# Projecting tokens 256 to 768 before their root is known, in a one-core hybrid encoder layer

## The chip, the cores and the metric

The kernel runs as one program on one core of a Trainium2 chip. The metric is the device time of one execution in microseconds (us); lower is better. The engines are named as in the profile: PE (TensorE, matrix products; PEld is its loading of weights), DVE (VectorE), ACT (ScalarE), POOL (GpSimd) and SP (SyncE, which here issues DMAs).

## What is computed

The reference is one encoder layer over two sequences with the same weights: 256 tokens of a prompt and 1024 tokens of a sample, 1280 in all, 1024 features each. The part around the change is the first step of the layer, the normalisation and the first projection:

```python
def rmsnorm(x, w):
    xf = x.astype(F32)
    y = xf * lax.rsqrt(jnp.mean(xf * xf, axis=-1, keepdims=True) + EPS)
    return (y * w.astype(F32)).astype(x.dtype)

h = rmsnorm(x, pre_mix_norm)
z = h @ w_in + b_in
aq, ak, av, mq, mk, mv, mo, mi, mf, gates = jnp.split(z, SPLIT_POINTS, axis=-1)
ya = windowed_gqa_attention(aq, ak, av, attn_sink)
ym = bidirectional_mlstm(mq, mk, mv, mo, mi, mf, mlstm_norm)
```

Behind it follow a gated merge of both branches, an output projection with a second norm, and a gated feed-forward network with a short convolution. Since the root of a token is one factor for all its features, `rmsnorm(x) @ w` is the same as `(x * w_norm) @ w` times the root of that token; the bias comes after.

## The kernel before

Tokens lie on the free axis and features on the partitions. The 1024 features are `KT = 8` tiles of 128. Every matrix product is made in two-part numbers: an operand is split into a high part (`unit_h`, `ht_h`) and what is left of it (`unit_l`, `ht_l`), and a product of one tile is three matmuls: high by high, low by high, high by low. Weights come in units of 128 output columns (512 KB, tile `unit_raw`), five slots of them, in which unit n lies in slot n mod 5. ACT makes a unit's high part (`unit_hi`, line 2030, semaphore `s_wh`) and POOL its low part (`take_low`, line 1396, semaphore `s_split`).

The program of every engine is an order written out by hand; engines meet only at semaphores. The tokens are worked in three chunks, `CHUNKS`: 0 is tokens 0 to 256, 1 is 256 to 768, 2 is 768 to 1280. The list `START` gives the order of the first groups on PE. For each chunk these are the gate columns of the mLSTM ("if", unit 0, 16 columns that count) and then the groups of units 1 to 4, which are the queries and keys of the first mLSTM head. A group's number is 3u + c for unit u + 1 and chunk c. In `if_group` the first of these groups (two in chunk 1) runs beside the gate columns, tile by tile, as the tiles of `ht` become ready. After `START` come the ten blocks of values and output gates (`vo_group`), 128 tokens each, whose moving operand is units 5 to 8 at once (slots 0 to 3), and which therefore need all four.

A chunk is prepared as follows. SP loads `xs`. ACT squares the eight tiles (`square_x`, line 2013), DVE adds the squares (lines 2422, 2429, 2432), PE sums them over the partitions with a matrix of ones (`sum_squares`, lines 3310 and 3314), ACT makes the root (`rstd_x`, lines 2018 and 2020). Then, tile by tile, DVE multiplies x by the norm's weight and the root (line 2477), ACT makes the high part `ht_h` (`x_hi`, line 2026), and DVE subtracts it to give `ht_l` (line 2482). `s_htd` counts the finished tiles.

After the third chunk DVE clears row tiles for the gate arithmetic (lines 2486 to 2492; these tiles share their memory with `xs`), adds up the gate rows of chunk 2 (`if_sum(2)`, line 2445), and goes on with the gates' scans. On SP the loads of units 5 and 6 wait only for a free slot, but those of units 7 and 8 stand behind the copies of the gate rows:

```python
m_first[4]()
m_first[5]()
sp.wait_ge(ev_dve, GROUPS[("if", 0, 2)][3])
sp.wait_ge(p_row, 1)
for d in range(2):
    sp.dma_start(r_li[32 * d:32 * d + 4, :], r_if[4 * d:4 * d + 4, :]).then_inc(p_in, 16)
    sp.dma_start(r_f[32 * d:32 * d + 4, :], r_if[8 + 4 * d:12 + 4 * d, :]).then_inc(p_in, 16)
for k in range(6, M_UNITS):
    m_first[k]()
```

(`m_first[k]` loads unit k + 1. `ev_dve` at that count is `if_sum(2)`, and `p_row` 1 is the last of the clears.) On ACT the high part of unit 8 stands behind that of unit 7, behind two activations of the gate rows (lines 2103 and 2105, which wait for DVE's line 2500), and behind one eviction. The first block of values waits with `pe.wait_ge(s_wh, M_UNITS)` for the high parts of all eight units.

Of the kernel before, what the change touches and what calls it, by code (L numbers as in the profile page):

```python
# [24 lines left out]
P = 128  # L25
# [140 lines left out]
HI_HEADS = M_UNITS + 4  # L166
# [40 lines left out]
START = [("if", 0, 0)] + [("M", 0, 3 * u) for u in range(4)]  # L207
START += [("if", 0, 1)] + [("M", 0, 3 * u + 1) for u in range(4)]
START += [("if", 0, 2)] + [("M", 0, 3 * u + 2) for u in range(4)]
START_BANKS = [0, 1, 5, 6, 7]  # L210

SUM_BEFORE = [9, 10]

BESIDE_IF = [[0], [1, 4], [2]]
# [209 lines left out]
def group_tables():  # L424

    order = list(START)
    out = {}
    for h in range(HEADS):
        order += [("M", h, g) for g in range(0 if h else 12, 22)]
        order += [("A", h, g) for g in (range(21) if h < HEADS - 1 else [*range(15), *LATE])]  # L430
    count = {"act": 0, "dve": 0}
    last = {}
    for i, key in enumerate(order):
        bank = START_BANKS[i % 5] if i < len(START) else i % 2
        eng = "dve" if key[0] == "if" or key[0] == "M" and key[2] >= 12 else "act"
# [23 lines left out]
def build(nc, w, wdn, xt, cols, bvo, sink, outs):  # L459
# [22 lines left out]
    unit_raw = at("unit_raw", 20480, [P, SLOTS, KT, P])  # L482

# [58 lines left out]
    sq_x = at("sq_x", 81920, [P, KT, T])  # L542
    ones0 = at("ones0", 196288, [P, P])
# [85 lines left out]
    s_xl = [sem(f"x_landed{c}") for c in range(3)]  # L629
    s_cols = sem("cols_landed")  # L630
    s_cst = sem("consts_dve")
# [10 lines left out]
    s_wh1 = sem("first_unit_hi")  # L642
# [259 lines left out]
    with ctx_block as block:  # L902
# [3 lines left out]
        def _(sp):  # L906
# [447 lines left out]
        def _(pool):  # L1354
            nc.gpsimd.memset(ident[:], 0.0)
# [26 lines left out]
            def take_rest(n, done, half):  # L1382
                slot = n % SLOTS
                pool.wait_ge(s_wh, M_UNITS + done)
# [6 lines left out]
            def take_low(n):  # L1391

                pool.wait_ge(*((s_wh1, 1) if n == 1 else (s_wh, n)))
                step = 2 if n < SLOTS else KT
                for k in range(0, KT, step):
# [5 lines left out]
            low = slice(HD, P)  # L1401
            nc.gpsimd.tensor_tensor(unit_h[:, 0, :, low], unit_raw[:, 0, :, low], unit_h[:, 0, :, low].bitcast(F32),
                                    ALU.subtract).then_inc(s_split, 1)
            for n in range(1, 1 + M_UNITS):
                take_low(n)
# [595 lines left out]
        def _(act):  # L2001
            nc.scalar.preload_act_table_set("natural_log_exp_and_others")

            act.dma_start(colt[:, 0:NCOL], cols[:]).then_inc(s_cols, 16)
            act.dma_start(sinks[:], sink[0:1, :].to_broadcast([P, 16])).then_inc(s_cols, 16)

            def square_x(c, k):
                a, b = CHUNKS[c]
                act.wait_ge(s_xl[c], 16)
                if c:  # L2010
                    act.wait_ge(s_sqm, c)
# [3 lines left out]
            def rstd_x(c):  # L2015
                stat = ps[:, 2 + c, 0:CHUNKS[c][1] - CHUNKS[c][0]]
                act.wait_ge(s_sqm, c + 1)
                nc.scalar.activation(stat, stat, ACT.Ln, bias=eps_col, scale=1.0 / D)
                act.drain()
                nc.scalar.activation(stat, stat, ACT.Exp, scale=-0.5).then_inc(s_rs, 1)  # L2020

            def x_hi(c, tiles=range(KT)):
                a, b = CHUNKS[c]
                for k in tiles:
                    act.wait_ge(s_xn, c * KT + k + 1)
# [21 lines left out]
            def evac_m(g, h, shift=0):  # L2047
# [17 lines left out]
            act.wait_ge(s_unit[2], 16)
            for k in range(4):
                x_hi(0, [k])
                last = nc.scalar.activation(unit_h[:, 2, 2 * k:2 * k + 2], unit_raw[:, 2, 2 * k:2 * k + 2], ACT.Identity)
            last.then_inc(s_wh, 1)
            x_hi(0, range(4, 7))  # L2070
            square_x(1, 0)
            x_hi(0, [7])
            square_x(1, 1)
            square_x(1, 2)
            unit_hi(3)
            for k in range(3, KT):
                square_x(1, k)
            unit_hi(4)
            act.wait_ge(s_cols, 32)
# [3 lines left out]
            rstd_x(1)  # L2083
            x_hi(1)
            evac_m(6, 0)
            evac_m(9, 0)
            for k in range(KT):
                square_x(2, k)
            evac_if(1)
            evac_m(1, 0)  # L2090
            evac_m(4, 0)
            rstd_x(2)
            evac_m(7, 0)
            x_hi(2)
            evac_m(10, 0)
# [23 lines left out]
            act.wait_ge(p_80, 32)  # L2119
# [291 lines left out]
        def _(dve):  # L2411
            V = nc.vector
            V.memset(ones0[:], 1.0)
            V.memset(eps_col, EPS).then_inc(s_cst, 1)
            for r in range(16):
                V.memset(slope8[:, r:r + 1], -(2.0 ** (-8.0 * (r + 1) / 16)) * HD ** 0.5)
            def add_squares_x(c):

                t = slice(CHUNKS[2][0], CHUNKS[2][0] + CHUNKS[c][1] - CHUNKS[c][0])
                for k in range(1, KT):  # L2420
                    dve.wait_ge(s_sq, c * KT + k + 1)
                    V.tensor_tensor(sq_x[:, 0, t], sq_x[:, 0, t], sq_x[:, k, t], ALU.add)
                    dve.drain()
                dve.sem_inc(s_sqa, 1)

            for k in range(0, KT, 2):
                dve.wait_ge(s_sq, k + 2)
                t = slice(CHUNKS[2][0], CHUNKS[2][0] + SEQ_A)
                V.tensor_tensor(sq_x[:, k, t], sq_x[:, k, t], sq_x[:, k + 1, t], ALU.add)
                if k % 4 == 2:  # L2430
                    dve.drain()
                    V.tensor_tensor(sq_x[:, k - 2, t], sq_x[:, k - 2, t], sq_x[:, k, t], ALU.add).then_inc(s_sqa, 1)
            dve.wait_ge(s_cols, 32)
# [7 lines left out]
            def if_sum(c):  # L2441
                a, b = CHUNKS[c]
                rows = slice(0, 4 * HEADS)
                dve.wait_ge(s_ifl, c + 1)
# [17 lines left out]
            for c, (a, b) in enumerate(CHUNKS):  # L2462
                if c:
                    add_squares_x(c)
                    if_sum(c - 1)
                if c == 1:
                    dve.wait_ge(s_cstp, 1)

                    V.scalar_tensor_tensor(absrel[:], absrel[:], -1.0, absrel[:], ALU.mult, ALU.max)
                    dve.drain()  # L2470
                    V.tensor_scalar(y_st.rearrange("p a b t -> p (a b t)")[:, 0:3 * P], absrel[:], float(P), BIG, ALU.is_gt, ALU.mult)
                    dve.drain()
                    V.tensor_tensor(absrel[:], absrel[:], y_st.rearrange("p a b t -> p (a b t)")[:, 0:3 * P], ALU.max)
                dve.wait_ge(s_rs, c + 1)
                for k in range(KT + 1):
                    if k < KT:
                        V.scalar_tensor_tensor(xs[:, k, a:b], xs[:, k, a:b], colt[:, C_PRE + k:C_PRE + k + 1],
                                               ps[:, 2 + c, 0:b - a], ALU.mult, ALU.mult).then_inc(s_xn, 1)
                    if k:

                        dve.wait_ge(s_xh, c * KT + k)
                        V.tensor_tensor(ht_l[:, k - 1, a:b], xs[:, k - 1, a:b], ht_h[:, k - 1, a:b].bitcast(F32),
                                        ALU.subtract).then_inc(s_htd, 1)

# [115 lines left out]
            def gated(i, h):  # L2600
# [11 lines left out]
                last.then_inc(m_ss, 1)  # L2612

# [657 lines left out]
        def _(pe):  # L3271
# [31 lines left out]
            pe.wait_ge(s_cst, 1)  # L3303
            def sum_squares(c):
                a, b = CHUNKS[c]
                first = CHUNKS[2][0]
                if c == 0:
                    for p in range(2):
                        pe.wait_ge(s_sqa, p + 1)
# [3 lines left out]
                pe.wait_ge(s_sqa, 2 + c)  # L3313
# [769 lines left out]
```

## Time and profile before

| | before |
|---|---|
| median of 3 runs | 2379.15 us (2378.35 to 2379.68) |
| span of the profiled execution, first to last instruction | 2375.6 us |
| PE busy | 2342.6 us, 99% of the span |
| DVE, POOL, ACT busy | 65%, 54%, 38% of the span |
| PE's longest idle stretches | 8.83 us at the start, 2.73 us before the first projection |

The page gives the profiled execution's time as its span alone; the median of the runs lies 3.55 us above it. The chain of work that ended last is PE for 88% of the span. All that the change touches lies in the first 145 us.

### The profile page before, as it was taken

To read this page: it belongs to the slowest core of one execution; us is meant where nothing else is said; L and a number is where in the kernel's file an instruction comes from. 1 tells how busy PE (TensorE), PEld (TensorE's weight loads), DVE (VectorE), ACT (ScalarE), POOL (GpSimd) and SP (SyncE) were. 2 spreads that over 40 slices of the span, in tenths; PEclk is the share of its full clock that TensorE was granted. 3 is DMA by queue.
4 is the path that set the end of the run, shared out by engine and by line. 5 is a ranking of instruction groups with operands and counts; after the bars stand their busy time and mean duration, and the time that the engine had idled before them with its cause. 6 is when DMAs were issued, how large, how long until landed. Compare 5 with 4: busy or idle time off the path is not lost.

```text
span 2375.6 us, 37136 instructions
## 1 busy us (share of the span) xinstructions
PE 2342.6 (99%) x13734; PEld 2120.7 (89%) x13734; DVE 1546.4 (65%) x2699; ACT 909.6 (38%) x1862; POOL 1279.8 (54%) x1556
## 2 busy tenths in 40 slices
PE   7999999999999999999999999999999999999998
PEld 6888888888888888888888899999999999989887
DVE  6734467554674547755786642999778777965447
ACT  5212443224442244324644112554333434552443
POOL 3365522555225641346452548797455555986576
PEclk9999999999999999999999999999999999999999
DMA  3133211321113311223454443332443434488873
GB/s 139 52 104 94 69 38 27 109 92 54 36 40 99 102 52 32 70 79 123 128 169 158 138 155 117 122 122 89 153 147 131 165 130 138 144 279 271 282 238 120
DMA packets 186956, 285.66 MB, mean 120 GB/s; under 512 B 14344, under 2 KB 126824, under 8 KB 186776
## 3 DMA queue, kind: packets, MB, share of 16 engines
q1 hardware_dynamic: 139320, 241.99, 30.7%
q10 hardware_dynamic: 47456, 41.31, 5.9%
q8 instruction: 109, 1.79, 0.3%
q14 instruction: 71, 0.58, 0.1%
HBM read 203.48 MB, written 79.68 MB: 119 GB/s over the span
## 4 chain that ended last, share of the span: by engine, by line
PE 88%; DVE 5%; DVEq 2%; POOL 2%; ACT 1%; DMA 1%; issue 1%; ACTq 0%; POOLq 0%
PE ps L3285 15%; PE ps L3287 15%; PE ps L3286 15%; PE ps L3840 4%; PE ps L3842 4%; PE ps L3841 4%; PE ps L3352 3%; PE ps L3350 3%; PE ps L3351 3%; PE ps L3300 3%; PE ps L3296 3%; PE ps L3297 3%; PE ps L3549 2%; PE ps L3457 2%; PE ps L3569 2%; PE ps L3583 1%
## 5 line engine op out<-in xcount | busy, mean ns | idle before, releaser
L3285 PE MATMUL ps<-ht_h,unit_h 128*128 128x512 f32 (+1 forms) x1408 | 503.7, 358 | 0.8 <-POOL unit_l L1396 0.6
L3287 PE MATMUL ps<-ht_h,unit_l 128*128 128x512 f32 (+1 forms) x1408 | 498.4, 354 | 0.0
L3286 PE MATMUL ps<-ht_l,unit_h 128*128 128x512 f32 (+1 forms) x1408 | 498.1, 354 | 0.0
L1374 POOL TENSOR_TENSOR unit_h<-unit_raw,colt 128x256 fp32r<-128x256 f32 x320 | 208.5, 683 | 275.1 <-DMA unit_raw<-w 274.8
L3285 PEld LDWEIGHTS ps<-ht_h,unit_h 128*128 128x128 f32 x1408 | 266.2, 189 | 37.2 <-POOL unit_l L1396 1.6
L3287 PEld LDWEIGHTS ps<-ht_h,unit_l 128*128 128x128 f32 x1408 | 265.9, 189 | 37.4
L3286 PEld LDWEIGHTS ps<-ht_l,unit_h 128*128 128x128 f32 x1408 | 266.2, 189 | 35.1 <-issue 0.2
L1378 POOL TENSOR_TENSOR unit_l<-unit_raw,unit_h 128x256 fp32r<-128x256 f32 x320 | 246.8, 803 | 11.7 <-issue 0.4
L1546 POOL TENSOR_TENSOR unit_l<-unit_raw,unit_h 128x256 fp32r<-128x256 f32 x164 | 157.8, 987 | 91.9 <-DVE unit_raw L2944 91.9
L1546 POOL TENSOR_TENSOR sum_l<-sum_raw,sum_h 128x256 fp32r<-128x256 f32 x132 | 138.9, 1073 | 91.9 <-DVE sum_raw L2951 78.6
L1467 POOL TENSOR_TENSOR v_high<-v_raw,colt 128x256 fp32r<-128x256 f32 x40 | 27.1, 677 | 231.3 <-DVE o_st L2459 231.3
L2273 ACT ACTIVATE prob<-prob,small 128x384 f32<-128x384 f32 (+1 forms) x160 | 89.8, 563 | 113.0 <-DVE small L2661 112.9
L1586 POOL TENSOR_TENSOR block_l<-block_raw,block_h 128x256 fp32r<-128x256 f32 x120 | 107.2, 933 | 45.5 <-ACT block_h L1899 45.5
L3296 PE MATMUL ps<-operands,unit_h 128*128 128x320 f32 (+1 forms) x420 | 125.5, 311 | 1.0 <-ACT kept_products L1819 1.0
L3297 PE MATMUL ps<-operands,unit_h 128*128 128x320 f32 (+1 forms) x420 | 124.9, 309 | 0.0
L2648 DVE SCALAR_TENSOR_TENSOR prob<-absrel,slope,ps 128x384 f32<-128x384 f32 (+1 forms) x160 | 79.0, 556 | 68.1 <-PE ps L3569 39.0
L3350 PE MATMUL ps<-unit_h,ht_h 128*128 128x512 f32 x312 | 123.2, 395 | 0.0
L3352 PE MATMUL ps<-unit_h,ht_l 128*128 128x512 f32 x312 | 121.6, 390 | 0.0
L3351 PE MATMUL ps<-unit_l,ht_h 128*128 128x512 f32 x312 | 121.5, 389 | 0.0
L1577 POOL TENSOR_TENSOR down_l<-down_raw,down_h 128x256 fp32r<-128x256 f32 x88 | 82.0, 967 | 33.3 <-DVE s_stage L3082 26.7
L3285 PE MATMUL ps<-operands,unit_h 128*128 128x322 f32 (+1 forms) x320 | 99.7, 311 | 0.3
L3287 PE MATMUL ps<-operands,unit_l 128*128 128x322 f32 (+1 forms) x320 | 99.5, 311 | 0.0
(417 smaller groups left out, 6463.7 us busy)
## 6 DMA issues: line engine op xcount, KB each, us to landing
unit_raw<-w SPq DMA_DIRECT2D x149, 512.0 KB, 4.0
bw<-exponent_rows_scratch ACTq DMA_DIRECT2D x40, 256.0 KB, 3.7
down_raw<-wdn SPq DMA_DIRECT2D x24, 384.0 KB, 4.1
side_raw<-side_sum_scratch SPq DMA_DIRECT2D x24, 384.0 KB, 5.9
block_raw<-weight_sum_scratch SPq DMA_DIRECT2D x16, 576.0 KB, 4.3
gate_scratch<-g_st SPq DMA_DIRECT2D x28, 256.0 KB, 3.6
stage<-f_scratch SPq DMA_DIRECT2D x28, 256.0 KB, 3.0
side_sum_scratch<-stage SPq DMA_DIRECT2D x14, 512.0 KB, 2.9
```

The lines of the kernel that those rows point to most:

```text
L1374: nc.gpsimd.tensor_tensor(unit_h[:, slot, k:k + 2], unit_raw[:, slot, k:k + 2], one_col.unsqueeze(2).to_broadcast([P, 2, P]), ALU.mult)
L1378: last = nc.gpsimd.tensor_tensor(unit_l[:, slot, k:k + 2], unit_raw[:, slot, k:k + 2], unit_h[:, slot, k:k + 2].bitcast(F32), ALU.subtract)
L1546: last = nc.gpsimd.tensor_tensor(lo[:, k:k + 2], raw[:, k:k + 2], hi[:, k:k + 2].bitcast(F32), ALU.subtract)
L1586: last = nc.gpsimd.tensor_tensor(blk_l[n][:, a:b], blk_raw[n][:, a:b], blk_h[n][:, a:b].bitcast(F32), ALU.subtract)
L3285: mm(out_ap, wh, hi(k + k_first), start=first and k == 0, stop=False, skip_group_check=skip)
L3286: mm(out_ap, wh, lo(k + k_first), start=False, stop=False, skip_group_check=skip)
L3287: ins = mm(out_ap, wl, hi(k + k_first), start=False, stop=last and k == kts - 1, skip_group_check=skip)
L3296: mm(out_ap, unit[0](k), hi(k), start=first and k == 0, stop=False, skip_group_check=skip)
L3297: mm(out_ap, unit[0](k), lo(k), start=False, stop=False, skip_group_check=skip)
L3350: mm(ps[:, bank, :], ht_h[:, k, t], unit_h[:, 0:4, k], start=k == 0, stop=False)
L3351: mm(ps[:, bank, :], ht_h[:, k, t], unit_l[:, 0:4, k], start=False, stop=False)
L3352: ins = mm(ps[:, bank, :], ht_l[:, k, t], unit_h[:, 0:4, k], start=False, stop=k == KT - 1)
```

## The change

Chunk 1 is now the first to be projected, then chunk 0, then chunk 2 (`RAW_FIRST`). Its tiles are loaded in four pairs, ahead of everything but the gate weights, and are split into high and low part without the root: x times the norm's weight only. The gate columns and groups 1, 4, 7 and 10 (`RAW_M`) are made from these raw tiles; DVE multiplies the root into them as it evicts them (`raw_m`, `raw_if`) and ACT adds the bias afterwards (`raw_bias`). The squares of chunk 1 and 0 are added by DVE as before, in tiles of their own for chunk 1; those of chunk 2 are added by POOL. The normalised split of chunk 1, which the blocks of values and everything later read, is made after that of chunk 2 (`normed(1)` behind `normed(2)`). The gate weights are loaded as 16 columns per tile instead of 128. The core of the diff:

```diff
+HI_START = M_UNITS + 1
+RAW_FIRST = [1, 0, 2]
+NORMED = {0: 1, 2: 2, 1: 3}
+START = []
+for _c in RAW_FIRST:
+    START += [("if", 0, _c)] + [("M", 0, 3 * u + _c) for u in range(4)]
+RAW_M = [1, 4, 7, 10]
+SUM_BEFORE = {7: 1, 10: 0, 6: 2}
+BESIDE_IF = [[0], [1], [2]]
...
+            def load_first(n):
+                a, b = CHUNKS[1]
+                sp.dma_start(xs[:, 2 * n:2 * n + 2, a:b], xt[2 * n:2 * n + 2, :, a:b].rearrange("k p t -> p k t")
+                             ).then_inc(s_xf[n], 16)
+            sp.dma_start(if_raw[:], w[0, :, 0:KT * 4 * HEADS].rearrange("p (k c) -> p k c", k=KT)
+                         ).then_inc(s_unit[0], 16)
+            load_first(0)
+            m_first[0]()
+            for n in range(1, 4):
+                load_first(n)
+            m_first[1]()
             load_x(0)
-            load(lambda hh: 0, 0)
-            m_first[0]()
-            m_first[1]()
-            load_x(1)
             m_first[2]()
             m_first[3]()
             load_x(2)
...
+            third = slice(CHUNKS[2][0], T)
+            for k in range(1, KT):
+                pool.wait_ge(s_sq, 2 * KT + k + 1)
+                nc.gpsimd.tensor_tensor(sq_x[:, 0, third], sq_x[:, 0, third], sq_x[:, k, third], ALU.add)
+                pool.drain()
+            pool.sem_inc(s_sqa, 1)
...
+            def raw_hi(k):
+                a, b = CHUNKS[1]
+                act.wait_ge(s_xf[k // 2], 16 if k > 1 else 32)
+                nc.scalar.activation(ht_h[:, k, a:b], xs[:, k, a:b], ACT.Identity, scale=colt[:, C_PRE + k:C_PRE + k + 1]
+                                     ).then_inc(s_xh, 1)
...
+            rstd_x(1)
+            unit_hi(4)
             rstd_x(0)
+            for k in range(KT):
                 x_hi(0, [k])
+                square_x(2, k)
+            act.wait_ge(a_sel, 1)
+            for g in RAW_M:
+                raw_bias(g)
             evac_if(0)
             evac_m(0, 0)
             evac_m(3, 0)
+            rstd_x(2)
+            x_hi(2)
             evac_m(6, 0)
             evac_m(9, 0)
+            x_hi(1)
             evac_if(2)
             evac_m(2, 0)
             unit_hi(5)
...
+            for k in range(KT):
+                dve.wait_ge(s_xh, k + 1)
+                V.scalar_tensor_tensor(ht_l[:, k, first], xs[:, k, first], colt[:, C_PRE + k:C_PRE + k + 1],
+                                       ht_h[:, k, first].bitcast(F32), ALU.mult, ALU.subtract).then_inc(s_htd, 1)
...
+            def raw_m(g):
+                u = g // 3
+                dve.wait_ge(d_done, GROUPS[("M", 0, g)][0] + 1)
+                V.scalar_tensor_tensor((mq_t if u < 2 else mk_t)[:, u % 2, first], ps[:, GROUPS[("M", 0, g)][1], :],
+                                       1.0 if u < 2 else DH ** -0.5, r_raw[:], ALU.mult, ALU.mult).then_inc(ev_dve, 1)
...
+            raw_if()
+            for g in RAW_M[:2]:
+                raw_m(g)
+            normed(0)
+            for g in RAW_M[2:]:
+                raw_m(g)
+            if_sum(0)
+            normed(2)
+            normed(1)
+            dve.wait_ge(s_cstp, 2)
...
-                    pe.wait_ge(s_wh, M_UNITS)
+                    pe.wait_ge(s_wh, HI_START)
...
+                if blk == 2 and h + shift == 0:
+                    pe.wait_ge(s_htd, 4 * KT)
```

Three places of the orders are shown. The first is DVE's program at the end of the preparation. In the kernel before, the last low part of chunk 2 is followed at once by the clears and by `if_sum(2)` (the `r_if` row; the row behind it waits for the copies of the gate rows):

```order
L2482 TENSOR_TENSOR ht_l<-xs,ht_h 128x512 x2
L2486 MEMSET v_high 128x10x2
L2487 MEMSET r_li 36x1280
L2488 MEMSET r_f 36x1280
L2489 MEMSET r_m 36x1280
L2490 MEMSET r_mp 36x10
L2492 MEMSET r_rst 36x1280
L2445 SCALAR_TENSOR_TENSOR r_if<-ps,colt,r_if 16x512
```

In the changed kernel the same clears and the same `if_sum(2)` on DVE stand behind the whole of `normed(1)`, of which the last two rows are shown (`r_raw` is the root of chunk 1), and behind the three operations on `absrel`:

```order
L2494 SCALAR_TENSOR_TENSOR xs<-xs,colt,r_raw 128x512
L2499 TENSOR_TENSOR ht_l<-xs,ht_h 128x512 x2
L2544 SCALAR_TENSOR_TENSOR absrel<-absrel 128x384
L2546 TENSOR_SCALAR y_st<-absrel 128x384
L2548 TENSOR_TENSOR absrel<-absrel,y_st 128x384
L2551 MEMSET v_high 128x10x2
L2552 MEMSET r_li 36x1280
L2553 MEMSET r_f 36x1280
L2554 MEMSET r_m 36x1280
L2555 MEMSET r_mp 36x10
L2557 MEMSET r_rst 36x1280
L2470 SCALAR_TENSOR_TENSOR r_if<-ps,colt,r_if 16x512
```

So 16 operations of 128x512 and the three on `absrel` now lie between the end of chunk 2's split and the gate rows; in the kernel before they were done ahead of chunk 2. The second place is SP's queue from its start, in the kernel before:

```order
L909 DMA xs<-xt 128x8x256
L917 DMA unit_raw<-w 128x1024 x3
L909 DMA xs<-xt 128x8x512
L917 DMA unit_raw<-w 128x1024 x2
L909 DMA xs<-xt 128x8x512
L967 DMA bias_vo<-bvo 128x512
L917 DMA unit_raw<-w 128x1024 x2
L973 DMA r_li<-r_if 4x1280
L974 DMA r_f<-r_if 4x1280
L973 DMA r_li<-r_if 4x1280
L974 DMA r_f<-r_if 4x1280
L917 DMA unit_raw<-w 128x1024 x2
```

In the changed kernel the head of SP's queue is another, up to the load of chunk 2; from `bias_vo` on the rows follow one another as before, units 7 and 8 again behind the four copies of the gate rows:

```order
L970 DMA if_raw<-w 128x128
L967 DMA xs<-xt 128x2x512
L923 DMA unit_raw<-w 128x1024
L967 DMA xs<-xt 128x2x512 x3
L923 DMA unit_raw<-w 128x1024
L915 DMA xs<-xt 128x8x256
L923 DMA unit_raw<-w 128x1024 x2
L915 DMA xs<-xt 128x8x512
```

Two tiles of chunk 1 now come second in the queue, and chunk 0 sixth. The third place is POOL's program after its constants, in the kernel before: the low part of the gate weights, of units 1 to 4 and of units 5 to 8, and then its work on the first values:

```order
L1402 TENSOR_TENSOR unit_h<-unit_raw,unit_h 128x8x64
L1396 TENSOR_TENSOR unit_l<-unit_raw,unit_h 128x256 x16
L1396 TENSOR_TENSOR unit_l<-unit_raw,unit_h 128x1024 x4
L1467 TENSOR_TENSOR v_high<-v_raw,colt 128x256
L1469 TENSOR_TENSOR v_low<-v_raw,v_high 128x256
```

In the changed kernel seven additions of squares stand between units 4 and 5 on POOL:

```order
L1416 TENSOR_TENSOR unit_h<-if_raw,unit_h 128x8x16
L1411 TENSOR_TENSOR unit_l<-unit_raw,unit_h 128x256 x16
L1423 TENSOR_TENSOR sq_x<-sq_x 128x512 x7
L1411 TENSOR_TENSOR unit_l<-unit_raw,unit_h 128x1024 x4
L1489 TENSOR_TENSOR v_high<-v_raw,colt 128x256
```

The seven additions of 128x512 are new to POOL; on DVE, which made them before, they are gone.

## Rows read from the trace of the kernel before

**Rows 1.** The page's first line.
```profile
span 2375.6 us, 37136 instructions
```

**Rows 2.** Timeline of PE: start, us, engine, line, operation, count, idle before and its releaser.
```profile
8.83 2.35 PE L3310 MATMUL ps<-sq_x,ones 128*128 128x256 f32 x4 [8.83 <-DVE sq_x L2432]
13.91 0.55 PE L3381 MATMUL ps<-ht_h,unit_h 128*128 128x256 f32 x1 [2.73 <-DVE ht_l L2482]
...
20.02 0.31 PE L3381 MATMUL ps<-ht_h,unit_h 128*128 128x256 f32 x1
...
20.52 1.12 PE L3398 MATMUL ps<-ht_h,unit_l 128*128 128x256 f32 x8
21.48 0.28 PE L3285 MATMUL ps<-ht_h,unit_h 128*128 128x256 f32 x1
...
52.80 1.02 PE L3314 MATMUL ps<-sq_x,ones 128*128 128x512 f32 x2
...
59.14 0.39 PE L3381 MATMUL ps<-ht_h,unit_h 128*128 128x512 f32 x1
...
84.53 0.39 PE L3340 MATMUL ps<-unit_h,ht_h 128*128 128x512 f32 x1
...
88.68 0.50 PE L3344 MATMUL ps<-unit_l,ht_h 128*128 128x512 f32 x1 [0.37 <-POOL unit_l L1396]
```

**Rows 3.** SP's queue: start, us of issue, line, DMA; units 7 and 8 last.
```profile
0.74 0.44 SPq L909 DMA_DIRECT2D xs<-xt  x1
...
71.99 0.74 SPq L973 DMA_DIRECT2D r_li<-r_if  x1
...
74.65 4.96 SPq L917 DMA_DIRECT2D unit_raw<-w  x2
```

**Rows 4.** Timeline of ACT: the high part of unit 8.
```profile
82.72 1.06 ACT L2030 ACTIVATE unit_h<-unit_raw 128x1024 fp32r<-128x1024 f32 x1
```

**Rows 5.** Timeline of DVE: `absrel`, chunk 2's split from first to last, `if_sum(2)`.
```profile
27.63 0.79 DVE L2469 SCALAR_TENSOR_TENSOR absrel<-absrel 128x384 f32<-128x384 f32 x1
...
29.29 0.56 DVE L2473 TENSOR_TENSOR absrel<-absrel,y_st 128x384 f32<-128x384 f32 x1
...
55.20 1.41 DVE L2477 SCALAR_TENSOR_TENSOR xs<-xs,colt,ps 128x512 f32<-128x512 f32 x2 [7.04 <-ACT ps L2020]
...
64.22 1.47 DVE L2482 TENSOR_TENSOR ht_l<-xs,ht_h 128x512 fp32r<-128x512 f32 x2
...
71.35 0.62 DVE L2445 SCALAR_TENSOR_TENSOR r_if<-ps,colt,r_if 16x512 f32<-16x512 f32 x1
```

**Rows 6.** DMA issues of the page (KB each, us to landing), then of the first 90 us.
```profile
unit_raw<-w SPq DMA_DIRECT2D x149, 512.0 KB, 4.0
...
xs<-xt SPq DMA_DIRECT2D x1, 1024.0 KB, 5.6
```

**Rows 7.** Groups by shape, ACT's high part of a 512-wide tile: busy, mean ns.
```profile
L2026 ACT ACTIVATE ht_h<-xs 128x512 fp32r<-128x512 f32 x16 | 10.1, 632 | 8.9 <-DVE xs L2477 8.8
```

**Rows 8.** Timeline of DVE: chunk 0's split, additions of squares beside POOL and alone.
```profile
12.21 0.87 DVE L2477 SCALAR_TENSOR_TENSOR xs<-xs,colt,ps 128x256 f32<-128x256 f32 x2 [0.74 <-ACT ps L2020]
...
18.16 1.43 DVE L2482 TENSOR_TENSOR ht_l<-xs,ht_h 128x256 fp32r<-128x256 f32 x2
...
21.23 5.47 DVE L2422 TENSOR_TENSOR sq_x<-sq_x 128x512 f32<-128x512 f32 x5 [0.27 <-ACT sq_x L2013]
...
42.01 5.30 DVE L2422 TENSOR_TENSOR sq_x<-sq_x 128x512 f32<-128x512 f32 x7 [1.08 <-ACT sq_x L2013]
```

**Rows 9.** Timeline of POOL from 10 to 29 us.
```profile
10.15 1.29 POOL L1402 TENSOR_TENSOR unit_h<-unit_raw,unit_h 128x512 fp32r<-128x512 f32 x1 [7.43 <-ACT unit_h L2030]
11.40 2.96 POOL L1396 TENSOR_TENSOR unit_l<-unit_raw,unit_h 128x256 fp32r<-128x256 f32 x4
15.86 3.45 POOL L1396 TENSOR_TENSOR unit_l<-unit_raw,unit_h 128x256 fp32r<-128x256 f32 x4 [1.50 <-ACT unit_h L2068]
20.76 8.24 POOL L1396 TENSOR_TENSOR unit_l<-unit_raw,unit_h 128x256 fp32r<-128x256 f32 x8 [1.44 <-ACT unit_h L2030]
```

More of the change, by code:

```diff
@@ L434, in group_tables @@
         bank = START_BANKS[i % 5] if i < len(START) else i % 2
-        eng = "dve" if key[0] == "if" or key[0] == "M" and key[2] >= 12 else "act"
+        raw = key[1] == 0 and key[2] in RAW_M
+        eng = "dve" if key[0] == "if" or key[0] == "M" and (key[2] >= 12 or raw) else "act"
         count[eng] += 1
@@ L2460, in evac_vo, with normed @@
                                 ALU.add).then_inc(ev_dve, 1)
[L2462 to L2474, printed above, removed]
+            def normed(c, between=None):
+                a, b = CHUNKS[c]
+                root = r_raw[:] if c == 1 else ps[:, 2 + c, 0:b - a]
+                dve.wait_ge(s_rs, RAW_FIRST.index(c) + 1)
                 for k in range(KT + 1):
@@ L2483, in _, with raw_if @@
                                         ALU.subtract).then_inc(s_htd, 1)
+            def raw_if():
+                rows = slice(0, 4 * HEADS)
+                dve.wait_ge(s_ifl, 1)
+                V.tensor_tensor(r_if[rows, first], ps[rows, GROUPS[("if", 0, 1)][1], :], r_if[rows, first], ALU.add)
+                dve.wait_ge(s_rs, 1)
+                dve.drain()
+                V.tensor_tensor(r_if[rows, first], r_if[rows, first], r_raw[rows], ALU.mult)
+                dve.drain()
+                V.tensor_scalar(r_if[rows, first], r_if[rows, first], colt[rows, C_IF:C_IF + 1], None, ALU.add
+                                ).then_inc(ev_dve, 1)
@@ new lines, in _ @@
+            dve.sem_inc(s_sqa, 1)
+            for k in range(0, KT, 2):
+                dve.wait_ge(s_sq, KT + k + 2)
+                t = slice(CHUNKS[2][0], CHUNKS[2][0] + SEQ_A)
+                V.tensor_tensor(sq_x[:, k, t], sq_x[:, k, t], sq_x[:, k + 1, t], ALU.add)
+                if k % 4 == 2:
+                    dve.drain()
+                    V.tensor_tensor(sq_x[:, k - 2, t], sq_x[:, k - 2, t], sq_x[:, k, t], ALU.add).then_inc(s_sqa, 1)
+            raw_if()
+            for g in RAW_M[:2]:
+                raw_m(g)
@@ L2612, in gated @@
                 last.then_inc(m_ss, 1)
+            dve.wait_ge(p_80, 48)
             def mlstm(h, dense):
@@ L3399, in if_group @@
                     ins.then_inc(d_done, 1)
-            sum_squares(0)
+                    return
+                for k in range(KT):
+                    pe.wait_ge(s_htd, KT * NORMED[c] + k + 1)
+                    gates(k)
+                    beside_hi(k)
+                    ins = mm(beside, wl(k), ht_h[:, k, a:b], start=False, stop=k == KT - 1)
+                ins.then_inc(d_done, 1)
             for kind, _, g in START:
@@ L3996, in sl @@
         return slice(a, a + P)
-    gates = np.zeros((D, P), w_in.dtype)
-    for first in (0, HD):
-        gates[:, first:first + 4 * HEADS] = w_in[:, off_if:off_if + 4 * HEADS]
-    units = [unit(gates, slice(0, P))]
+    gates = np.zeros((P, KT * P), w_in.dtype)
+    gates[:, 0:KT * 4 * HEADS] = (w_in[:, off_if:off_if + 4 * HEADS].reshape(KT, P, 4 * HEADS).transpose(1, 0, 2)
+                                  .reshape(P, KT * 4 * HEADS))
+    units = [gates]
     for h in range(HEADS):
```

202 lines of the change are left out of this document (98 added, 104 removed).

## The prediction

> **What bounds the kernel now.** I read the page first: PE is busy nearly throughout a span of 2375.6 us [rows 1], so only two things can move the time here: work taken off PE, of which the change takes none (112 projection matmuls per chunk before and after), and time in which PE waits or runs slowly. Next I read PE's own timeline of the first 90 us. It waits 8.83 us for the squares of chunk 0 and 2.73 us more for the first split tile. The first projection starts at 13.91 us, and the next 28 matmuls of 256 columns take 0.218 us each, up to 20.02 us; from there eight take 0.96 us, 0.12 each [rows 2]. 256 columns in 0.21 us is the lower of TensorE's two clock levels, 1.2 GHz, in 0.11 the upper, 2.4 GHz. So the start costs 13.9 us of idleness, and a slow stretch of 6.1 us, half of which (3.05 us) is lost. After that PE is nearly always fed: chunk 2 runs its 112 matmuls from 59.14 to 84.53 us, 0.2267 each, and the first block of values follows at once, with one wait of 0.37 us [rows 2].
>
> Then I looked at what has to be there at 84.53. The first block needs the high part of units 5 to 8; that of unit 8 is ready at 82.72 + 1.06 = 83.78 [rows 4], only 0.75 us early. It is last on ACT behind the gate rows, and its load is last on SP behind their copies, which start at 71.99 [rows 3], as `if_sum(2)` ends on DVE (71.35 + 0.62 = 71.97) [rows 5]. So there is a chain of 83.78 - 71.97 = 11.81 us from `if_sum(2)` to the first block, and in the kernel before it was nearly the bound. This is the place that decides.
>
> **The change, part by part.** *The start.* The first pair of raw tiles is 512 KB. A lone load of that size lands after 4.0 us and one of 1 MB after 5.6 [rows 6], 1.6 us per further 512 KB. It is second in the queue, after the first issue at 0.74 of 0.44 us [rows 3], with 64 KB of gate weights and the column constants beside it, for which I add 0.5: it lands at about 5.7. ACT's high part takes 0.63 [rows 7], DVE's low part 0.7 (half of 1.41 for two of that shape) [rows 5]. PE starts at about 7.1 instead of 13.91. The other tiles come in faster (two per 1.6 us) than a cold PE uses them (four matmuls of 0.43 each), so they don't hold it.
>
> *Chunk 1.* Up to the sum for chunk 0 stand 88 matmuls (19.95 us), the sum for chunk 1 (0.9, from a row of 1.02 whose end overlaps), that for chunk 0 (about 1.0: a row of 2.35 in the slow stretch, halved and cut in the same way), and the slow start, which I take as long as in the row, 3.05 lost: 7.1 + 19.95 + 0.9 + 1.0 + 3.05 = 32.0. Group 10 ends 24 matmuls later, at 37.4.
>
> *Chunk 0.* DVE starts its split 1.03 us after the sum (8.83 + 2.35 to 12.21) [rows 2, 8], at 33.0. In the row its eight tiles end after 7.38 us (18.16 + 1.43) [rows 8], which would be ahead of PE. But POOL now adds the squares of chunk 2 meanwhile: seven additions of 128x512, 1.29 us each by the nearest row alone [rows 9]. What DVE and POOL do to each other can be read: POOL's 128x256 pieces take 0.74 us beside an idle DVE, 0.86 beside DVE's split, 1.03 beside DVE's additions, and DVE's additions of 128x512 take 0.76 (5.30 for 7) with POOL idle and 1.09 (5.47 for 5) with POOL at work [rows 8, 9]. POOL's two sizes give 0.55 us of transfer per 256 elements and 0.19 around it; 0.55 + 0.53 for DVE's 512 elements is the 1.09 of the row: they take turns. So one low part (about 0.35) waits for one addition (1.10): with a little between, 1.5 us a tile. The additions can start when two squares are there (two times 0.9 after a first 0.5), at 35.3; tile 2 is ready at 36.9, tile 7 at 44.4. PE, free at 37.4, finishes tile 7 at 45.0, group 3 (24 x 0.12) at 47.9 and the sum for chunk 2 at **E = 48.8**. If they did not take turns, PE would come through at 45.1 and E would be 46.0; I take the first, since both rows fit it, and keep the other as the lower end.
>
> The Trainium skill, "SBUF — State Buffer", section "Who interferes with whom", says that a VectorE instruction with two inputs in SBUF and a GpSimd instruction that reads SBUF exclude one another for a whole instruction. The 1.09 us agrees. By that rule E is 48.8, without it 46.0: it speaks against moving these additions to POOL.
>
> *From E on.* PE still has groups 6 and 9 (48 x 0.12) and the 112 matmuls of chunk 2 (25.4): 31.15 us, so it is through at 80.0, 4.5 us earlier than 84.53. DVE starts the split of chunk 2 1.38 us after the sum (52.80 + 1.02 to 55.20) and needs 10.49 us for it (to 64.22 + 1.47 = 65.69) [rows 2, 5]. Then it now makes the split of chunk 1, the same 16 operations, another 10.49 (its root comes from SBUF, not PSUM; no row shows that form in this width, and I take the same). Then `absrel`, 2.22 (27.63 to 29.29 + 0.56). Then the clears and `if_sum(2)`, 6.28 (65.69 to 71.97) [rows 5]. They cannot go ahead of it, since the cleared rows lie in the memory of `xs`. So `if_sum(2)` ends at 48.8 + 1.38 + 20.98 + 2.22 + 6.28 = **79.7**, 7.7 us later than before. Behind it wait on SP the four copies and the loads of units 7 and 8 (whose slots are free long before), on ACT the gate rows and the high part of unit 8, and on PE the first block. With the same 11.81 us that block starts at **91.5**, not 84.53: 6.95 us late. PE is idle for 11.5 us before it.
>
> *The clock.* The only such idleness in the trace is that of the start, and PE came out of it at the lower level. I take the same 6.1 us again, 3.05 lost. If the clock held, the block's 16 high-part matmuls would take 3.6 us, while unit 8's low part is ready 88.68 - 83.78 = 4.9 us after its high part [rows 2, 4]: a wait of 1.2 us. So this term is 3.05 or 1.2, and the old wait of 0.37 is gone in either case. The Trainium skill, "TensorE: Matmul & The Clock Gate", section on the HAM clock gate, says that the slow level is the default and activity releases it; no row here shows it for an idle stretch in mid-kernel.
>
> *Hidden at no cost.* Four evictions with the root on DVE (0.7 each), two of them between the splits of chunk 0 and 2, are over by 46 while DVE waits until 50; without that cover 1.4 us. Four bias activations and the gate rows' extra operations lie beside PE's work likewise. The second split is over at 71, far ahead of the third block of values that waits for it. Later consumers of the gate rows are delayed less (7.7) than PE, so they keep their distance.
>
> **Sum.** 6.95 + 3.05 - 0.37 = 9.6 us, nothing behind it gives it back as PE is the chain. Span 2385.2; the runs' median lies 3.55 above the span, so **2388.8 us**, 0.4% slower.
>
> **Rivals.** *The start's gain is kept.* If units 7 and 8 came in time, PE would enter the first block at 80.0: 4.5 us faster, 2374.6, or with E = 46.0 7.3 us, 2371.8. For it speaks that units 5 and 6 and all slots are indeed early; it decides once `if_sum(2)` ends by 80.0 - 11.8 = 68.2, which is 11.5 us earlier than worked out, more than the whole second split (10.5). Chance 0.05. *Neither contention nor a slow second start.* E = 46.0 gives the first block at 88.7, 4.15 late, and 1.2 - 0.37 for the low part: 5.0 us, 2384.1. If the first slow stretch is also half as long, 1.5 less: 2382.6, inside 0.2%. Chance 0.20, of which 0.15 falls inside. *POOL is slower still.* At 2.06 us per addition (twice 1.03 [rows 9]) the sum for chunk 2 waits until 49.7, E is 50.6, and the time 2390.6. Chance 0.14. *The raw tiles come late.* If the pair lands only with two further loads (3.2 us), everything shifts by that: 2392.0. Chance 0.06. My forecast has the remaining 0.55.
>
> **The numbers.** I call 0.2% (4.8 us) what this kernel's runs can tell from no change; they spread by 1.3 us. Slower by more: 0.55 + 0.05 + 0.14 + 0.06 = 0.80. Within: 0.15. Faster: 0.05. The range reaches from the low case inside 0.2% (2382.6) to the late tiles: 2382.5 to 2392.
>
> **What would show it.** In the changed kernel's timeline: PE's first projection near 7 us, without one of the two waits of before; the seven additions on POOL at 1.4 to 1.6 us each, with DVE's low parts of chunk 0 between them; PE through with chunk 2 near 80; `if_sum(2)` ending near 79.7, SP's copies right behind it, and one wait of PE of about 11 us, released by ACT's high part of unit 8, and slow matmuls behind it. I am wrong if that wait is short: if `if_sum(2)` ends before 70, or if the first block does not stand behind unit 8. A first projection later than 9 us would break the first step, and a sum for chunk 2 done by 46 that of POOL and DVE taking turns.

## The result and the profile after

The changed kernel takes 2387.62 us (median of 4 runs, 2386.28 to 2390.09), the kernel before, measured beside it, 2379.41 (2378.35 to 2379.98): 1.0038 times as long, 95% interval 1.0026 to 1.0049. It is 8.2 us slower; 2388.8 was predicted.

The page's first line, beside [rows 1], and the waits of PE in the first 100 us (releaser, us in total, times, longest):

```profile
span 2384.5 us, 37150 instructions
...
PE ps L3417 <- ACT unit_h L2055: 10.5, 1, 10.5
PE ps L3453 <- DVE ht_l L2457: 9.2, 1, 9.2
PE ps L3453 <- DVE ht_l L2499: 1.7, 3, 0.6
```

In the first block of values, where the kernel before waited 0.37 us, stands a wait of 10.5. PE's timeline, which answers to [rows 2]:

```profile
9.20 0.77 PE L3453 MATMUL ps<-ht_h,unit_h 128*128 128x512 f32 x1 [9.20 <-DVE ht_l L2457]
...
12.64 0.40 PE L3453 MATMUL ps<-ht_h,unit_h 128*128 128x512 f32 x1
...
44.82 0.39 PE L3453 MATMUL ps<-ht_h,unit_h 128*128 128x256 f32 x1 [0.56 <-DVE ht_l L2499]
...
48.39 1.02 PE L3385 MATMUL ps<-sq_x,ones 128*128 128x512 f32 x2
...
80.19 0.39 PE L3354 MATMUL ps<-ht_h,unit_l 128*128 128x512 f32 x1
91.08 0.77 PE L3417 MATMUL ps<-unit_h,ht_h 128*128 128x512 f32 x1 [10.50 <-ACT unit_h L2055]
...
94.54 0.39 PE L3417 MATMUL ps<-unit_h,ht_h 128*128 128x512 f32 x1
...
96.38 1.98 PE L3421 MATMUL ps<-unit_l,ht_h 128*128 128x512 f32 x8
```

The first projection starts 4.7 us earlier than before (9.20 for 13.91), the sum for chunk 2 comes 4.4 us earlier (48.39 for 52.80), and the last matmul of chunk 2 starts at 80.19, 4.1 us earlier (84.30 before). Then PE stands still, and the first block of values begins 6.55 us later than before (91.08 for 84.53). The rest of the chain tells why; this is the chain of work that ended last, cut to 70 to 100 us (start, us, what):

```profile
71.08 0.69 DVE ht_l L2499
...
76.40 1.12 DVE r_m L2554
...
79.03 0.55 DVE r_if L2470
79.60 0.74 SPq L987
...
82.26 3.56 DMA unit_raw<-w
85.84 1.06 ACT unit_h L2055
86.90 1.18 ACT r_b L2139
88.15 1.27 ACT r_b L2141
89.42 0.57 ACT mk_t L2062
89.99 0.95 ACT unit_h L2055
91.08 0.77 PE ps L3417
```

Read upwards: the block waits for the high part of unit 8 (89.99). That stands on ACT behind two activations of the gate rows and an eviction, those behind the high part of unit 7 (85.84); the loads of units 7 and 8 were issued on SP only behind the four copies of the gate rows; the copies waited for `if_sum(2)` (79.03); and `if_sum(2)` stands on DVE behind the clears and the end of the second split (71.08 + 0.69). From the end of `if_sum(2)` (79.57) to the end of that high part it is 89.89 + 1.04 - 79.57 = 11.4 us by ACT's timeline, nearly as long as before (11.81 by [rows 4, 5]).

### The profile page after: what moved, and what is told of

Its sections match the earlier page's. It is cut to its first block, busy times and chain, and to the rows that moved or that the text cites. A ratio compares the mean times of both kernels' runs of the same rounds, so it can differ in the third digit from the quotient of the medians.

```text
span 2384.5 us, 37150 instructions
## 1 busy us (share of the span) xinstructions
PE 2343.5 (98%) x13734; PEld 2121.5 (89%) x13734; DVE 1554.7 (65%) x2706; ACT 913.1 (38%) x1867; POOL 1289.1 (54%) x1564
## 4 chain that ended last, share of the span: by engine, by line
PE 89%; DVE 6%; DVEq 2%; POOL 1%; ACT 1%; DMA 1%; issue 0%; SPq 0%; ACTq 0%
PE ps L3352 15%; PE ps L3354 15%; PE ps L3353 15%; PE ps L3923 4%; PE ps L3924 4%; PE ps L3925 4%; PE ps L3367 3%; PE ps L3363 3%; PE ps L3364 3%; PE ps L3429 3%; PE ps L3431 3%; PE ps L3430 3%; PE ps L3632 2%; PE ps L3540 2%; PE ps L3652 2%; PE ps L3666 1%
## 5 line engine op out<-in xcount | busy, mean ns | idle before, releaser
L3352 PE MATMUL ps<-ht_h,unit_h 128*128 128x512 f32 (+1 forms) x1392 | 497.3, 357 | 0.3 <-issue 0.3
L3354 PE MATMUL ps<-ht_h,unit_l 128*128 128x512 f32 (+1 forms) x1392 | 492.2, 354 | 0.0
L3353 PE MATMUL ps<-ht_l,unit_h 128*128 128x512 f32 (+1 forms) x1392 | 491.9, 353 | 0.0
L1393 POOL TENSOR_TENSOR unit_l<-unit_raw,unit_h 128x256 fp32r<-128x256 f32 x320 | 246.1, 799 | 11.4
L3110 DVE TENSOR_TENSOR side<-side_raw,side 128x1536 fp32r<-128x1536 f32 (+2 forms) x40 | 65.2, 1662 | 53.0 <-ACT side L1833 52.9
```

The lines of the kernel that those rows point to most:

```text
L1393: last = nc.gpsimd.tensor_tensor(unit_l[:, slot, k:k + 2], unit_raw[:, slot, k:k + 2], unit_h[:, slot, k:k + 2].bitcast(F32), ALU.subtract)
L3352: mm(out_ap, wh, hi(k + k_first), start=first and k == 0, stop=False, skip_group_check=skip)
L3353: mm(out_ap, wh, lo(k + k_first), start=False, stop=False, skip_group_check=skip)
L3354: ins = mm(out_ap, wl, hi(k + k_first), start=False, stop=last and k == kts - 1, skip_group_check=skip)
```

## The experiments

Three theories went into the first four runs. **A**, that of the prediction: the second split makes the gate rows late, and they hold up unit 8 in two queues, SP's (its load) and ACT's (its high part). **B**: SP's queue alone does it. **C**: the loss lies in the start, in DVE and POOL holding each other up, or in the clock. The kernel before was measured again beside the first four runs (26 executions) and beside the last four (28); its median is 2378.93 us both times. Each experiment starts from the changed kernel.

**Loads first.** Units 7 and 8 are loaded ahead of the copies.

```diff
+            for k in range(6, M_UNITS):
+                m_first[k]()
             sp.wait_ge(ev_dve, GROUPS[("if", 0, 2)][3])
...
-            for k in range(6, M_UNITS):
-                m_first[k]()
```

> The loads of units 7 and 8 are issued on SP ahead of the wait for the gate rows; nothing else is changed. Theory A (the late gate rows hold unit 8's high part on ACT as well, behind the two activations of the gate rows): the loads land near 75 and 79 us, but the first block of values still starts near 91 and the time stays within 1 us of the changed kernel's 2387.6. Rival B (the queue of loads on SP is what holds the block): the wait of 10.5 us shrinks to a few us and the time falls by 8 to 12 us, to about 2377. Rival C (the loss lies in the start, the contention or the clock): no change, and the wait stays as long.

Measured: 2387.17 us, 1.0036 times before (1.0023 to 1.0049), no gain. ACT's timeline of this run:

```profile
77.47 1.06 ACT L2055 ACTIVATE unit_h<-unit_raw 128x1024 fp32r<-128x1024 f32 x1
89.54 1.27 ACT L2139 ACTIVATE r_b<-r_b 36x1280 f32<-36x1280 f32 x1 [11.01 <-DVE r_b L2565]
90.88 1.27 ACT L2141 ACTIVATE r_b<-r_b 36x1280 f32<-36x1280 f32 x1
92.05 0.67 ACT L2062 ACTIVATE mk_t<-ps,hc 128x512 f32<-128x512 f32 x1
92.62 1.04 ACT L2055 ACTIVATE unit_h<-unit_raw 128x1024 fp32r<-128x1024 f32 x1
```

Unit 7 is through at 78.5. Then ACT is idle for 11.01 us, waiting for the gate rows, and unit 8 is behind them. PE's wait is 10.51 us. B falls: once the load is early, the second queue holds it as long. That SP's queue would hold the block by itself too is read from the chain above, not tried.

**Loads and unit 8.** Also on ACT, unit 8 goes ahead of the gate rows.

```diff
+            evac_m(8, 0)
+            unit_hi(8)
             act.wait_ge(p_row, 2)
             nc.scalar.activation(r_b[0:36], r_b[0:36], ACT.Exp, scale=-1.0)
...
-            evac_m(8, 0)
-            unit_hi(8)
             evac_m(11, 0)
```

> As e1, and on ACT the high part of unit 8 and one eviction are put ahead of the two activations of the gate rows. Theory A: the first block starts at about 80.4, as PE is through with chunk 2, without a slow stretch. But DVE evicts the first block only behind the gates' scans, at about 99 to 100, as in the changed kernel, so PE waits some 8 us before the third block, which needs that bank; net gain only 3 to 4 us, time about 2384. Rival B or C: if the gates' chain holds nothing else, the whole wait and the slow restart are saved, 12 us, time about 2375.5.

Measured: 2382.89 us, 1.0016 (1.0007 to 1.0026). The 10.5 us are gone: chunk 2 runs into the first block at 81.17 without a wait. Another wait has come, PE's waits from 78 us on in this run:

```profile
PE ps L3429 <- DVE o_st L2484: 6.6, 1, 6.6
```

The third block (98.80) needs a bank that DVE evicts only after the gate rows' scans, so the late rows hold PE in a third queue. Gained against the changed kernel: 4.7 us; the trace accounts for 10.5 - 6.6 = 3.9, since behind either wait eight or nine matmuls run at 0.43 us.

**Early evictions.** In addition, DVE evicts the first blocks between the steps of the gate rows.

```diff
+            evac_vo(0, 0)
             dve.wait_ge(p_act, 1)
...
             V.tensor_tensor_scan(r_b[0:4], r_rst[0:4], r_f[0:4], 0.0, ALU.mult, ALU.add)
+            evac_vo(1, 0)
...
-                evac_vo(n, 0)
+                evac_vo(n + 2, 0)
...
-            evac_vo(2, 0)
+            evac_vo(4, 0)
```

> As e2, and on DVE the evictions of the first five blocks of values are moved ahead between the gates' steps (the first one behind the step before the softplus, the second behind the first scan, and so on). Theory A: no wait at the first or third block; PE runs 10.7 us ahead of the changed kernel and saves the slow restart of 1.7, until the transposes in the last block, which need the gates' rows at about 133 while PE is there at about 129: a wait of 3 to 4 us. Net gain 8 to 9 us, time about 2379, equal to the kernel before. If the gates' chain were not the cause: no gain over e2.

Measured: 2376.37 us, 0.9987 (0.9977 to 0.9996). All waits of PE from 78 to 180 us in this run:

```profile
PE ps L3501 <- ACT decay L2157: 1.0, 1, 1.0
```

11.25 us less than the changed kernel; the trace accounts for 10.5 (wait) + 1.6 (slow matmuls behind it) - 1.0 = 11.1. The spans of the two profiled executions differ by less, 9.6 us, since the clock cost them different amounts elsewhere (the sum and the last section). With these three moves the change, second split and all, is 2.6 us faster than the kernel before. The moves were not tried on the kernel before, but there PE has only one wait of 0.4 us between 78 and 180 us for them to save.

**No second split.** The second split is left out, and the blocks of chunk 1 read raw tiles, without the root (`normed(1)`, its high parts and the wait for them are missing).

```diff
             normed(2)
-            normed(1)
```

> The changed kernel without the second, normalised split of tokens 256 to 768: DVE's 16 operations and ACT's 8 are left out, so all that follows reads the raw tiles of these tokens. Theory A: the gate rows of chunk 2 end 10.5 us earlier, near 69, the first block starts near 80.9 (69.1 + 11.8), PE waits under 1 us there, and the time falls by 11 to 12 us to about 2376, faster than the kernel before by the gain at the start. Rival C: the second split is hidden behind PE's work; leaving it out changes less than 2 us.

Measured: 2377.22 us, 0.9993 (0.9983 to 1.0002), 10.4 us less than the changed kernel. PE's waits from 78 us on:

```profile
PE ps L3418 <- POOL unit_l L1411: 1.1, 1, 1.1
PE ps L3414 <- ACT unit_h L2055: 0.2, 1, 0.2
```

`if_sum(2)` ends at 69.53 in this run, and the block follows chunk 2 with 0.23 us between. So the second split is the cause; the queues of the first three runs are how it reaches PE. C falls as the main cause, since neither the third nor the fourth run touched the start.

**One addition.** POOL makes only the last of the seven additions of squares (six squares are left out of the root of chunk 2).

```diff
-            for k in range(1, KT):
+            for k in range(KT - 1, KT):
```

> The changed kernel with only the last of POOL's seven square additions (six squares are left out of the root of chunk 2). Theory A says DVE's low parts of chunk 0 wait a whole POOL addition each: without six of them the tiles follow one another at about 0.85 us instead of 1.44, the last tile of chunk 0 is ready near 41.4 instead of 44.8, PE does not wait for it (it is through with the tiles at 42.8 instead of 45.4), and everything behind, the wait of 10.5 us for unit 8 included, comes 2.6 us earlier: about 2385.0, or 2384 where the clock had fallen after those waits. Rival (the two engines do not hold each other up): the tiles keep their spacing, the time stays within 0.7 of 2387.6.

Measured: 2384.78 us, 1.0027 (1.0017 to 1.0037), 2.8 us less than the changed kernel. DVE's low parts in the changed kernel beside POOL's seven additions, then in this run:

```profile
36.03 9.89 POOL L1423 TENSOR_TENSOR sq_x<-sq_x 128x512 f32<-128x512 f32 x7 [4.02 <-ACT sq_x L2038]
...
39.36 1.12 DVE L2499 TENSOR_TENSOR ht_l<-xs,ht_h 128x256 fp32r<-128x256 f32 x1
...
40.80 1.11 DVE L2499 TENSOR_TENSOR ht_l<-xs,ht_h 128x256 fp32r<-128x256 f32 x1
```
```profile
38.04 0.42 DVE L2499 TENSOR_TENSOR ht_l<-xs,ht_h 128x256 fp32r<-128x256 f32 x1
...
38.87 0.42 DVE L2499 TENSOR_TENSOR ht_l<-xs,ht_h 128x256 fp32r<-128x256 f32 x1
```

A low part takes 1.12 us beside the additions and 0.42 without; tiles come every 1.44 or every 0.83 us. The rule of the Trainium skill that the prediction weighed ("SBUF — State Buffer", "Who interferes with whom") holds in this place too. So this part of C is real, but small beside the second split: 2.8 us, as much as lay between the prediction's two cases for E (48.8 and 46.0).

**Gates sooner.** The early evictions, and the gate rows' chain shortened: `absrel` ahead of both splits, two row clears on POOL.

```diff
+            pool.wait_ge(s_htd, 4 * KT)
+            nc.gpsimd.memset(r_li[0:36], 0.0)
+            nc.gpsimd.memset(r_f[0:36], 0.0).then_inc(s_cstp, 1)
...
-            V.memset(r_li[0:36], 0.0)
-            V.memset(r_f[0:36], 0.0)
```

> The variant with the early evictions, and in it the three operations on absrel ahead of both splits and two of the row clears on POOL. Theory A (the chain of the gate rows is what is late): the sum of the gate columns of chunk 2 ends about 4.5 us earlier (near 77 in that variant's own profile), and the only wait that PE has left behind the start, 1.0 us at the transposes for ACT's decay, goes: about 2375.4, 1.0 less than the variant without. Rival B (the clears hold up POOL's low parts of units 5 to 8): a new wait of 1 to 2 us at the low part of the first block, 2377 to 2378. Rival C (what is left has nothing to do with the gate rows): no difference, 2376.4.

Measured: 2375.17 us, 0.9984 (0.9975 to 0.9993). `if_sum(2)` ends 5.7 us earlier, at 76.64, but the wait that this was to remove is still there:

```profile
PE ps L3504 <- ACT decay L2160: 0.9, 1, 0.9
```

The 1.2 us less than the run before it therefore come from no mechanism I named, and the executions of the two (2374.06 to 2376.14, 2373.49 to 2378.14) overlap: inconclusive. Of the 5.7 us, 1.7 lie ahead of the edit (the sum for chunk 2 comes at 49.44 here and at 51.15 in the profile of the run before). The other 4.0 are used up again: DVE's first step on the rows, 0.82 us in the run before, takes 2.96 here, beside POOL's low parts; the copies are waited for 0.8 us longer; and DVE now waits 1.45 us for PE's blocks, whose evictions stand between the steps. So in this order PE's own blocks hold up the gate rows in part, and ACT's `decay` comes only 1.8 us earlier (131.23 for 133.02).

**Early squares.** As the last, and the squares of chunk 2 are made before the root of chunk 0; DVE adds three of them ahead of its split, POOL the rest.

```diff
             unit_hi(4)
+            for k in SQUARES_2:
+                square_x(2, k)
             rstd_x(0)
-            for k in range(KT):
-                x_hi(0, [k])
-                square_x(2, k)
+            x_hi(0)
```

> As the run with the gates sooner, and the squares of chunk 2 are made before the root of chunk 0 on ACT (those of chunk 0 lie in columns 0 to 256 of their tile for it), DVE adds three of them before its split of chunk 0, POOL the rest. If DVE and POOL hold each other up, only the first four tiles of chunk 0 are slowed, while PE is still at group 10; the last is ready near 42.8 instead of 44.8, PE's three waits of 0.57 go or shrink below 0.3 each, and with them the fall of the clock that followed them in some profiles: 2.0 us less than the run with the gates sooner, 3.4 less in such executions, about 2373. Rival: PE then waits as long at the first block or the transposes, since the gate rows come no earlier: no difference.

Measured: 2373.83 us, 0.9980 (0.9971 to 0.9989), 1.3 us less. PE's three waits of 0.57 have shrunk to one:

```profile
PE ps L3465 <- DVE ht_l L2504: 0.3, 1, 0.3
```

The sign was right and the size (2.0) too large: 1.7 - 0.3 = 1.4 us of waiting was all that there was to save.

**Matmuls of ones first.** As the last, and 19 matmuls of 128 columns of ones ahead of the first projection, in a bank that is written afresh later.

```diff
+            pe.wait_ge(s_sqa, 1)
+            for _ in range(19):
+                mm(ps[:, 4, 0:P], ones0[:], ones0[:], start=True, stop=True)
             for kind, _, g in START:
```

> As the run with early squares, and 19 matmuls of 128 columns of ones on PE ahead of the first projection, into a bank that is written afresh later. If the slow stretch of 3.4 to 6.0 us behind the first projection is PE's clock not yet granted, PE works through it on these and the projections start at the higher level: 1.7 to 3.0 us less, about 2370.5, with first matmuls of 0.21 to 0.23 us spacing instead of 0.43. Rival (the slow matmuls have another cause, such as the loads that share the memory, or the clock falls again in the gap before the first tile): still 0.43, no difference, or 1 us more if the matmuls of ones outlast the wait for the first tile.

Measured: 2372.72 us, 0.9974 (0.9964 to 0.9984), 1.1 us less than early squares. PE's timeline:

```profile
1.06 6.34 PE L3499 MATMUL ps<-ones 128*128 128x128 f32 x38 [1.06 <-DVE ones L2454]
9.36 0.47 PE L3465 MATMUL ps<-ht_h,unit_h 128*128 128x512 f32 x1 [1.96 <-DVE ht_l L2462]
...
10.50 0.40 PE L3472 MATMUL ps<-ht_h,unit_h 128*128 128x512 f32 x1
10.73 0.39 PE L3473 MATMUL ps<-ht_l,unit_h 128*128 128x512 f32 x1
...
12.07 0.50 PE L3465 MATMUL ps<-ht_h,unit_h 128*128 128x512 f32 x1 [0.48 <-DVE ht_l L2462]
```

The matmuls of ones (38 in the profile, two for each) run ahead of the tiles, and those of 512 columns now follow at 0.23 us wherever their tile is there, where they took 0.43. The loads are as busy as before (a DMA share of 1.04 to 1.07 from 9 to 12 us, 1.04 to 1.08 in the changed kernel), so they did not make the slow stretch: it hangs on what PE did before, as its clock does in the windows further below. The 1.96 us of idleness between did not bring the slow stretch back. But PE is then faster than the tiles: it waits for DVE's low parts (0.48 at 12.07, smaller gaps behind), so not all of the expected 1.7 to 3.0 us comes through. The 1.1 us between the medians are themselves uncertain: the executions (2370.80 to 2375.29, 2372.51 to 2375.22 for early squares) overlap, and in the two profiles, where early squares had a short slow stretch of 3.5 us, the gain at the end of the first 32 matmuls is 0.26 us (18.14 for 18.40). Against both kernels the gain is clear: this version is 6.2 us under before.

## Why the prediction was right

**What decides.** The step that `if_sum(2)` moves behind a second split, and the first block with it, was right in each link: end of `if_sum(2)` 79.57 (79.7 predicted), block 91.08 (91.5), wait 10.5 (11.5), released by ACT's high part of unit 8. That 79.57 lies so near is partly luck: E came 0.5 us late, and `absrel`, the clears and `if_sum(2)` took 7.8 us (71.78 to 79.57) instead of 8.5. DVE's timeline, which answers to [rows 5]:

```profile
50.80 1.41 DVE L2494 SCALAR_TENSOR_TENSOR xs<-xs,colt,ps 128x512 f32<-128x512 f32 x2 [3.17 <-ACT ps L2045]
...
61.20 1.41 DVE L2494 SCALAR_TENSOR_TENSOR xs<-xs,colt,r_raw 128x512 f32<-128x512 f32 x2
...
70.31 1.47 DVE L2499 TENSOR_TENSOR ht_l<-xs,ht_h 128x512 fp32r<-128x512 f32 x2
...
78.95 0.62 DVE L2470 SCALAR_TENSOR_TENSOR r_if<-ps,colt,r_if 16x512 f32<-16x512 f32 x1
```

The two splits take 10.4 and 10.6 us (10.49 each predicted). The first and the fourth run show the rest of the step: the queues hold PE, and without the split they don't.

**The start.** 7.1 was predicted for the first projection, 9.20 measured: by the prediction's own sign (later than 9) its first step broke, if narrowly. The mis-sized term is the landing of the first pair: ACT's high part, which waits for it (the column constants had landed 2.3 us after their issue), starts at 7.47, so the pair lands 6.3 us after its issue, not 4.5. I priced it from a lone load and left out the loads issued behind it. In the first 30 us the four pairs took more than twice the 4.0 us of [rows 6] (KB each, median us from issue to landing):

```profile
xs<-xt SPq DMA_DIRECT2D x4, 512.0 KB, 8.3
```

That they share the DMA engines with those loads is argued, not tried. The slow stretch went the other way: 9.20 to 12.64, eight matmuls at 0.43, 1.6 us lost for 3.05. The two errors nearly cancel, which is luck: DVE's split of chunk 0 starts at 33.67, 33.0 predicted. The column of the granted clock does not show this stretch; of 9 to 11 us it says 1.00 (its us; busy us and instructions of PE, PEld, DVE, ACT, POOL; the granted clock; DMA share and GB/s):

```profile
9.00:11.00 2.00, 1.80 (x4) 1.49 (x5) 0.88 (x3) 1.71 (x3) 1.14 (x2) 1.00 1.07 408
```

The kernel before has 1.00 in its slow stretch as well. That the clock is at its lower level there rests on the spacing, which is that of the matmuls at a granted 0.50 below, and on the run with the matmuls of ones.

**Chunk 0.** Taking turns was right in place and size: a tile every 1.44 us (1.5), POOL's seven additions in 9.89 us, 1.41 each, E at 49.3 (48.39 + 0.9; 48.8 predicted).

**The clock behind the wait.** Predicted 3.05 lost, measured 1.6. Windows behind the wait, with the columns of the window above:

```profile
90.00:92.00 2.00, 0.92 (x2) 0.83 (x3) 1.93 (x2) 1.98 (x3) 0.98 (x1) 0.50 0.00 0
92.00:94.00 2.00, 2.00 (x6) 1.54 (x5) 1.99 (x2) 0.81 (x1) 2.00 (x1) 0.50 0.03 8
94.00:96.00 2.00, 2.00 (x9) 1.61 (x9) 2.00 (x1) 0.00 (x0) 2.00 (x1) 0.89 0.00 0
```

The clock was at 0.50, the lower level, until 94.5; so it is at that level behind 10.5 us of idleness in mid-kernel, which no row of before could show. The Trainium skill's "TensorE: Matmul & The Clock Gate", section on the HAM clock gate, by which the slow level is the default, agrees. Eight matmuls took 0.43 us instead of 0.23. That is 1.4 us under the term; the block's low part, weighed as its other case, was not waited for (POOL ends it at 96.01, PE reads it at 96.38).

**The sum.** 6.55 + 1.6 - 0.37 = 7.8 us by the terms as measured, 9.6 predicted, 8.9 between the spans and 8.2 between the medians. So the terms were 1.8 us too high, 1.4 of it the slow stretch behind the wait, for which I took the length seen in one execution. The rest of the spans' difference lies far behind. PE is 7.56 us later than before at the transposes of the gate columns (141.72 for 134.16) and 7.18 at 2096.87 (2089.69 before), where both kernels have just waited 2.25 us for a low part of POOL. Behind this wait the granted clock falls in the changed kernel's profile and not in that of before; first the changed kernel, then the one before:

```profile
2098.00:2100.00 2.00, 2.00 (x12) 2.00 (x12) 0.12 (x1) 1.99 (x3) 2.00 (x3) 0.51 1.08 361
```
```profile
2091.00:2093.00 2.00, 2.00 (x15) 1.83 (x14) 0.09 (x1) 1.99 (x3) 2.00 (x4) 1.00 1.05 358
```

By 2104.79 (2096.05 before) PE is 8.74 us later. Whether the change brings this fall on stays open: of the profiles of the eight experiments six show it and two don't, and of the kernel before there is one. With this 1.6 us, which no term of the prediction stands for, the forecast of the span is only 0.7 us high (2385.2 for 2384.5), and that of the median 1.2, as the median lies 3.1 us above the span instead of 3.55. That it came so near is partly luck.

## What to carry over

When work is moved on an engine, list what is queued behind it on every engine, not only on its own: here one split on an engine that was 65% busy held up a load, an activation and an eviction, and each had to be moved before the gain at the start showed. Moving a wait's last link alone may give nothing; a run in which the suspected work is left out gives the bound. And a queue that holds an unrelated load behind a wait is worth reordering even where it costs nothing today: [rows 4] had 0.75 us left.

## What was not expected of the hardware

*The slow stretch at the start has no fixed length.* The same first matmuls run at 0.43 us for 3.4 us in the changed kernel, 6.0 in the run with loads first and in that with early evictions, 4.8 with loads and unit 8 moved, 4.0 without the second split. One execution is no measure of it: it moves everything behind by up to 1.3 us.

*Three short waits, and the clock may fall or not.* In the run with loads first (and alike in that with early evictions) PE waits three times 0.57 us for tiles of chunk 0, and then the granted clock drops. Windows of that run, with the columns of the windows above:

```profile
42.00:44.00 2.00, 1.43 (x10) 1.15 (x10) 2.00 (x4) 1.29 (x4) 1.86 (x2) 1.00 0.02 4
44.00:46.00 2.00, 0.99 (x7) 0.66 (x5) 2.00 (x2) 1.81 (x4) 1.72 (x3) 0.98 0.00 0
46.00:48.00 2.00, 1.86 (x8) 1.87 (x9) 1.28 (x3) 1.28 (x2) 1.22 (x1) 0.50 0.00 0
48.00:50.00 2.00, 2.00 (x13) 2.00 (x13) 0.47 (x1) 0.90 (x3) 0.00 (x0) 0.67 0.00 0
```

From the last of these waits to the sum for chunk 2 it is 4.98 us there and 3.57 in the changed kernel, in whose profile the same three waits left the clock at 1.00, as they did in the runs with loads and unit 8 moved, without the second split and with the gates sooner. So the same code can lose 1.4 us more or not. That the waits bring the fall on is likely, not shown: it came behind them in two of six profiles, and in none of the three that have at most one of them.
